# Moving two of sixteen gate blocks from the prompt's part of a decoder layer into the sample's attention

## The chip, the cores and the metric

The kernel runs on one NeuronCore of a Trainium2 chip. The metric is the device time of one execution in microseconds; the kernel before took 1476.8 us (median of three runs, 1475.82 to 1482.26). Engines are called PE (matrix products), DVE (vector), ACT (scalar functions), POOL and SP; in this kernel SP only issues transfers (DMAs), and POOL issues the gathers.

## The reference, cut to what matters

One layer of a decoder is applied to a prompt (256 tokens) and to a sample group (8 sequences of 4 new tokens with 1024 tokens of cache each) with the same weights. The part that matters here:

```
h  = rms_norm(x) * (1 + scale) + shift            # 288 rows of 1024
q, kc, vc, ks, vs, kw, vw, g_nsa, hq, hf, hi, hg, ga, gb = split(h @ w_in)
o_nsa = sparse attention: compressed, selected and window branches, mixed by g_nsa
o_hg  = HGRN2 (4 heads, 128 x 128 state)
m     = sigmoid(ga) * (o_nsa @ w_branch_a) + sigmoid(gb) * (o_hg @ w_branch_b)
out   = m @ w_out
```

After it stand the norm, the residual and a mixture of 32 experts, 4 for each token, whose weights (192 pieces of 2 MB) are all streamed from HBM.

`ga` and `gb` are 1024 columns each. The kernel computes them transposed, in sixteen blocks of 128 columns: block n is `w_in[:, columns of block n]^T @ h^T`, a result of 128 x 288.

## The kernel before, in words

All instructions of each engine are written out in order; engines wait for each other by counting semaphores. What follows is in the order of time.

**Front.** The projection of all columns but `ga` and `gb`, and the compressed keys.

**The sample's attention.** PE transposes cached keys through two banks of PSUM (6 and 7, the "ring", lines 928 to 938) and ACT copies them out. Window scores come first, then selected scores (line 971), which use banks 1 to 4. The selected rows of the cache are gathered by POOL; the last of eight gathers (batch 7, line 2571) waits for `pv_ps` 2, that is, for the window values, because it overwrites a place that the window used. DVE then adds biases and takes maxima, group by group (`softmax`, line 2103; group 0 reads banks 2 and 4 and then raises `s_max` to 4), ACT takes exponentials, DVE divides (`probs` 3), and PE transposes the probabilities (`probs_T`, line 985, five steps) and multiplies them with the cached values (`cached_values`, line 1008) in lines 1104 to 1108. In front of the first of these transposes `probs_T` has `keep_clock`, ten products of the identity with constants whose result nobody reads (line 989).

**The prompt sweep.** A planner in Python (`prompt_steps`, line 165) lays out the steps of the prompt's attention (twelve units), of its HGRN (two tiles of 128 tokens) and of gate blocks into one order, `PROMPT_STEPS`, from assumed durations. Each engine issues its own steps in that order. A gate block is two half blocks of four products each; all go to bank 7. The blocks that the planner finishes before the last other step are `INSIDE` (0 to 9), the rest `LEFT` (10 to 15).

**The tail.** PE runs the blocks in `LEFT` between the steps of the sample's HGRN (lines 1256 to 1286): one block after the inputs, one after the transposes of the keys, one after the heads, one between the two halves of the state updates, and the others after them. Then come two steps of the attention branch (line 1294), the transposes of the HGRN result, and the merge of eight steps (line 1300), after which DVE writes `mT`. SP starts the stream of expert weights when all of `mT` is there (line 704).

**Weights of the gate blocks.** SP loads one piece of 1024 x 128 values (512 KB) for each block, into two places in turn (`load_gate`, line 641); from the third piece on it waits until the block two before has been computed (`gate_ps`). The first twelve are issued in one loop (line 647). Inside it, after the piece of block 5, SP issues a copy of 4064 KB from HBM to HBM, the window state shifted by four tokens (line 650). The remaining pieces are issued between the loads of the branch weights (line 674). SP takes its instructions in order, so a wait there holds all later loads.

Of the kernel before, what the change touches and what calls it, by code (L numbers as in the profile page):

```python
# [20 lines left out]
ACT = mybir.ActivationFunctionType  # L21
# [3 lines left out]
P = 128  # L25
D = 1024
KD = D // P
TP, NB, TS = 256, 8, 4
NS = NB * TS
# [15 lines left out]
ZW = OFF["ga"]  # L45
NZ = -(-ZW // 512)
NGATE = 2 * D // P
# [114 lines left out]
    return sum((i + 1 if branch else 1) for i, branch, _ in UNITS[:u])  # L162


def prompt_steps():


# [24 lines left out]
    for i in range(2):  # L192
# [20 lines left out]
        step("dve", 2.0, "gated", (i,), ("rms", (i,)))  # L213
        step("pe", 1.0, "out", (i,), ("gated", (i,)), ("out_T", (i - 1,)))
        step("act", 0.5, "out_T", (i,), ("out", (i,)))
    for j in range(NGATE):
        for half in range(2):
            step("pe", 2.0, "gates", (j, half), *([("gates", (j, 0))] if half else [("gates_out", (j - 1,))] if j else []))
        step("act", 0.5, "gates_out", (j,), ("gates", (j, 1)))
    emptied = {("out", (i,)): ("out_T", (i,)) for i in range(2)}  # L220
    emptied.update({("gates", (j, 0)): ("gates_out", (j,)) for j in range(NGATE)})
    bank7 = []
    free, done, order = {"pe": 0.0, "act": 0.0, "dve": 0.0}, {}, []
    while todo:
# [14 lines left out]


PROMPT_STEPS = prompt_steps()
_end = max(n for n, s in enumerate(PROMPT_STEPS) if s[0] not in ("gates", "gates_out"))
INSIDE = [j for j in range(NGATE) if PROMPT_STEPS.index(("gates_out", (j,))) < _end]
LEFT = [j for j in range(NGATE) if j not in INSIDE]
PROMPT_STEPS = [s for s in PROMPT_STEPS if s[0] not in ("gates", "gates_out") or s[1][0] in INSIDE]
ORDER = (2, 0, 1)
PIECES = 6 * E
# [2 lines left out]
def build(nc, A, O):  # L250

    with ExitStack() as ctx:
# [207 lines left out]
        osq = ftake(512, HH, DK)  # L460
        sP = [ftake(4 * 256, 4, 256) for _ in range(2)]
        pTp = [ftake(2 * 4 * P, 2, 4, P) for _ in range(2)]
        gate_piece = [ftake(D, KD, P) for _ in range(2)]
        fr["at"] = work0 + 1536 + 512 * 2 + P + 512
        s0 = ftake(NB * HH * DK, NB * HH, DK)
        vm = ftake(NB * DK, NB, DK)
# [102 lines left out]
        def _(sp):  # L569
# [66 lines left out]
            sp.dma_start(lb, A["hg_lb_logits"][0:1].broadcast_to([P, 512])).then_inc(S("ld_hg"), 16)  # L636
            sp.dma_start(oml, A["hg_lb_logits"][1:2].broadcast_to([P, 512])).then_inc(S("ld_hg"), 16)

            sp.wait_ge(S("pv_ps"), 3)
            sp.dma_start(hgn, A["hg_norm"][0:1].broadcast_to([P, P])).then_inc(S("ld_hgn"), 16)  # L640
            def load_gate(j):
                if j >= 2:
                    sp.wait_ge(S("gate_ps"), j - 1)
                sp.dma_start(gate_piece[j % 2], w_in[:, ZW + P * j:ZW + P * j + P].rearrange("(k p) c -> p k c", p=P)
                             ).then_inc(S(f"ld_gp{j % 2}"), 16)

            for j in range(min(NGATE, len(INSIDE) + 2)):
                load_gate(j)
                if j == 5:
                    sp.dma_start(O[7][0, :, 0:WIN - TS].rearrange("b t k g d -> b (t k g d)"),  # L650
                                 A["state_win"][0, :, TS:WIN].rearrange("b t k g d -> b (t k g d)")).then_inc(S("st_out"), 16)
# [1 line left out]
            sp.wait_ge(S("state"), 2)  # L653
            sp.dma_start(s0, A["state_hgrn"][0].rearrange("b h k v -> k (b h) v")).then_inc(S("ld_s0"), 16)
            sp.dma_start(O[8][0, 0].rearrange("h k v -> k h v"), state).then_inc(S("st_state"), 16)
            if len(INSIDE) + 2 < NGATE:
                load_gate(len(INSIDE) + 2)
# [15 lines left out]

            for k in range(8):
                load_branch(k)
                if len(INSIDE) + 3 + k < NGATE:
                    load_gate(len(INSIDE) + 3 + k)
# [68 lines left out]
        def _(pe):  # L746
            mm = nc.tensor.matmul

            def keep_clock(bank, n):

                for _ in range(n):
                    mm(bank[:, 0:256], ident, ctab[:, 0:256], start=True, stop=True)
# [232 lines left out]
            def probs_T(what, n, done):  # L985

                bank = to_ring(what, n)
                if (what, n) == ("sel_p", 0):
                    keep_clock(bank, 10)
                pe.wait_ge(S("probs"), done)  # L990
                src, w, tiles = {"cmp": (sSc, NCMP, 1), "win_p": (sSw, WIN_W, 5), "sel_p": (sSs, SEL_W, 9)}[what]
                for t in range(2 * n, min(2 * n + 2, tiles)):
                    c = min(P, w - P * t)
                    for g in range(G):
                        last = nc.tensor.transpose(bank[0:c, 256 * (t % 2) + P * g:256 * (t % 2) + P * g + P],
                                                   src[:, g, P * t:P * t + c], ident)
                last.then_inc(S("tr_ps"), 1)
# [97 lines left out]
            for i in range(2):  # L1095
                bank = to_ring("pq", 2 * i)
                for r in range(R):
                    last = nc.tensor.transpose(bank[:, P * r:P * r + P], z[:, i, P * r:P * r + P], ident)
                last.then_inc(S("tr_ps"), 1)
                bank = to_ring("pq", 2 * i + 1)  # L1100
                for n, name in enumerate(("ks", "kw")):
                    last = nc.tensor.transpose(bank[:, P * n:P * n + P], zc(i, name, P), ident)
                last.then_inc(S("tr_ps"), 1)
            for t in range(5):
                probs_T("sel_p", t, 3)
                if t:
                    cached_values("sel_p", t - 1)
            cached_values("sel_p", 4)
# [4 lines left out]

            pe.wait_ge(S("tr"), len(RING))
            pe.wait_ge(S("scores_in"), 2)

            def scores(u):
                i, branch, rp = UNITS[u]
# [89 lines left out]
            outs_before = [sum(place_of[("out", (i,))] < place_of[("gates", (j, 0))] for i in range(2)) for j in INSIDE] + [2] * len(LEFT)  # L1208
            gates_before = [sum(place_of[("gates", (j, 0))] < place_of[("out", (i,))] for j in INSIDE) for i in range(2)] + [NGATE]

            def gate_block(j, half):

                if half == 0:
                    pe.wait_ge(S(f"ld_gp{j % 2}"), 16 * (j // 2) + 16)
                    if j:
                        pe.wait_ge(S("gate_out"), j)
                    if outs_before[j]:
                        pe.wait_ge(S("ohT"), outs_before[j])
                for k in range(4 * half, 4 * half + 4):
                    last = mm(banks[7][:, 0:TP + NS], gate_piece[j % 2][:, k], hT[:, k], start=k == 0, stop=k == KD - 1)  # L1220
                if half:
                    last.then_inc(S("gate_ps"), 1)

# [326 lines left out]
        def _(act):  # L1550
# [32 lines left out]
            def exps(src, width, groups, seq):  # L1583
                act.wait_ge(S("s_max"), seq)
                for g in groups:
                    last = fn(src[:, g, 0:width], src[:, g, 0:width], ACT.Exp, bias=sa_max[:, g:g + 1], accum_out=sa_sum[:, g:g + 1])
                last.then_inc(S("s_exp"), 1)
# [92 lines left out]
                nc.scalar.copy(kT[:, :, P * i:P * i + P], bank[:, 0:256].rearrange("p (n t) -> p n t", n=2)).then_inc(S("tr"), 1)  # L1680
            exps(sSs, SEL_W, (0,), 4)
            exps(sSs, SEL_W, (1,), 5)
            for t in range(5):
                probs_out("sel_p", t, 2)
            act.wait_ge(S("pv_ps"), 3)
            nc.scalar.copy(o_ev[:, 0], banks[0][:, 0:P]).then_inc(S("oS"), 1)
            for n in range(2):
                bank = from_ring("out", n)
                for g in range(G):
                    last = fn(onT[DH * g:DH * g + DH, :, 256 + 16 * n:272 + 16 * n].rearrange("p r (b t) -> p r b t", t=TS),  # L1690
                              bank[DH * g:DH * g + DH, 0:P].rearrange("p (b g r t) -> p g r b t", b=4, g=G, r=R)[:, g],
                              ACT.Copy, scale=0.5)
                last.then_inc(S("tr"), 1)
# [64 lines left out]
            def hgrn_result_out(i):  # L1758
# [5 lines left out]
            def gates_out(j):  # L1764
                act.wait_ge(S("gate_ps"), j + 1)
                fn(gates[:, j], banks[7][:, 0:TP + NS], ACT.Tanh, scale=0.5).then_inc(S("gate_out"), 1)
# [844 lines left out]
```

## Time and profile before

| | |
|---|---|
| median of three runs | 1476.8 us |
| profiled execution: its own time | 1477.04 us |
| its span | 1475.2 us |
| PE busy | 1292.9 us |
| DVE / ACT busy | 397.5 / 257.1 us |
| moved by DMA | 503.98 MB |
| mean granted PE clock | 0.954 |

Times in the rows are microseconds from the start of the span. The sample's attention fills roughly 235 to 305, the prompt sweep 305 to 406, the tail 406 to 474, routing and the experts the rest. Where a row names an engine at the end in brackets with an arrow, that is what ended the idle time before the row.

### The profile page before, as it was taken

Reading aid. Unit: us, or ns where it says so; the run is one execution under the profiler, and the core shown is the slowest. Engines: PE = TensorE matmul, PEld = TensorE weight load, DVE = VectorE, ACT = ScalarE, POOL = GpSimd, SP = SyncE. Lnnn points to the kernel's source line nnn. Section 1 sums busy time; section 2 is a strip of 40 time slices with the busy share of each in tenths; the row PEclk is TensorE's granted clock in tenths of the full one; section 3 lists DMA queues with packets and bytes.
Section 4 is the critical chain, followed back from the end, with each engine's and each line's share of the span. In section 5 each row is a group of like instructions: output and inputs, shape, how many; then the busy total and the mean of one; then the engine's idle time right before and its main releaser. Section 6 shows DMA issues by size and latency. Waiting matters only on the chain.

```text
span 1475.2 us, 32485 instructions
## 1 busy us (share of the span) xinstructions
PE 1292.9 (88%) x14329; PEld 639.3 (43%) x14329; DVE 397.5 (27%) x991; ACT 257.1 (17%) x618; POOL 32.1 (2%) x50
## 2 busy tenths in 40 slices
PE   5899998799989978899999679999998669797685
PEld 4554555466767433344444224444443123242232
DVE  5320012458743551112121102121211011121012
ACT  5100005556520310001010001010100000000001
POOL 2000003100000000000000000000000000000000
PEclk9899999999999989899999989999999789899897
DMA  9985764224297999999999999699999999999996
GB/s 283 328 305 200 265 231 168 68 60 156 61 260 254 377 378 424 424 423 426 426 424 422 425 425 425 273 420 414 424 424 425 422 425 425 426 422 424 426 425 252
DMA packets 99043, 503.98 MB, mean 342 GB/s; under 512 B 9473, under 2 KB 38937, under 8 KB 63938
## 3 DMA queue, kind: packets, MB, share of 16 engines
q1 hardware_dynamic: 95234, 483.47, 82.4%
q0 software_dynamic: 3520, 18.90, 3.7%
q8 instruction: 83, 1.36, 0.4%
q10 hardware_dynamic: 192, 0.13, 0.0%
q14 instruction: 14, 0.11, 0.0%
HBM read 496.33 MB, written 10.31 MB: 343 GB/s over the span
## 4 chain that ended last, share of the span: by engine, by line
PE 64%; DMA 26%; DVE 3%; SPq 2%; ACT 2%; issue 1%; POOL 0%; DVEq 0%; ACTq 0%
PE psum L1444 18%; DMA arena<-in_w_up 12%; DMA arena<-in_w_down 11%; PE psum L1463 9%; PE psum L811 4%; PE psum L1220 3%; PE psum L1051 3%; PE psum L1052 3%; PE psum L1477 3%; PE psum L1416 2%; PE psum L1317 2%; PE psum L1430 2%; DMA arena<-in_cache_cmp,arena 2%; SPq L702 2%; PE psum L824 1%
## 5 line engine op out<-in xcount | busy, mean ns | idle before, releaser
L1444 PE MATMUL psum<-arena 128*32 128x512 f32 x3328 | 407.3, 637 | 110.3 <-DMA arena<-in_w_up 95.2
L1444 PEld LDWEIGHTS psum<-arena 128*32 128x32 f32 x3328 | 114.8, 113 | 371.2 <-issue 288.2
L2493 DVE TENSOR_SCALAR arena<-psum 128x256 f32<-128x256 f32 x52 | 22.2, 426 | 678.6 <-PE psum L1430 678.6
L1463 PE MATMUL psum<-arena 128*32 128x256 f32 x3328 | 192.7, 381 | 7.7 <-DMA arena<-in_w_down 7.7
L1463 PEld LDWEIGHTS psum<-arena 128*32 128x32 f32 x3328 | 101.6, 110 | 75.7 <-DMA arena<-in_w_down 12.8
L1880 ACT ACTIVATE arena<-arena 128x256 f32<-128x256 f32 x52 | 21.7, 418 | 572.7 <-DVE arena L2493 572.7
L1220 PE MATMUL psum<-arena 128*128 128x288 f32 x256 | 67.8, 410 | 3.5 <-DMA arena<-in_w_in 2.9
L1477 PE MATMUL psum<-arena 32*128 32x256 f32 x864 | 61.9, 399 | 1.1 <-ACT arena L1889 0.6
L811 PE MATMUL psum<-arena 64*128 64x504 f32 x256 | 56.8, 598 | 1.7 <-DVE arena L1959 1.7
L1430 PE MATMUL psum<-arena 32*32 32x512 f32 x416 | 57.6, 625 | 0.0
L1416 PE MATMUL psum<-arena 128*32 128x256 f32 x832 | 55.9, 386 | 0.0
L1884 ACT COPY arena<-psum 128x256 f32<-128x256 f32 x52 | 19.4, 374 | 203.9 <-PE psum L1463 203.9
L1051 PE MATMUL psum<-arena 128*128 128x512 f32 (+1 forms) x112 | 54.9, 571 | 0.0
L1220 PEld LDWEIGHTS psum<-arena 128*128 128x128 f32 x256 | 46.5, 189 | 18.7 <-DMA arena<-in_w_in 5.2
L1052 PE MATMUL psum<-arena 128*128 128x512 f32 (+1 forms) x112 | 54.1, 564 | 0.0
L1477 PEld LDWEIGHTS psum<-arena 32*128 32x128 f32 x864 | 39.0, 183 | 24.3 <-issue 22.1
L1416 PEld LDWEIGHTS psum<-arena 128*32 128x32 f32 x832 | 21.7, 109 | 52.2 <-issue 43.3
L811 PEld LDWEIGHTS psum<-arena 64*128 64x128 f32 x256 | 25.6, 192 | 30.6 <-issue 30.6
L1484 PE MATMUL psum<-arena 32*32 32x256 f32 x440 | 37.1, 408 | 0.0
L784 PE MATMUL psum<-arena 128*128 128x128 f32 x128 | 21.2, 327 | 16.2 <-DMA arena<-in_cache_cmp,arena 14.9
L1434 PE MATMUL psum<-arena 32*32 32x256 f32 x416 | 34.8, 405 | 0.0
L2065 DVE COPY arena<-psum 128x512 f32<-128x512 f32 (+1 forms) x7 | 4.6, 658 | 109.4 <-PE psum L1057 109.4
(458 smaller groups left out, 1319.5 us busy)
## 6 DMA issues: line engine op xcount, KB each, us to landing
arena<-in_w_up SPq DMA_DIRECT2D x128, 2048.0 KB, 31.7
arena<-in_w_down SPq DMA_DIRECT2D x64, 2048.0 KB, 26.4
arena<-in_w_ada SPq DMA_DIRECT2D x12, 2048.0 KB, 11.3
arena<-in_w_in SPq DMA_DIRECT2D x6, 2048.0 KB, 12.0
arena<-in_w_in SPq DMA_DIRECT2D x16, 512.0 KB, 4.1
arena<-in_state_win SPq DMA_DIRECT2D x4, 1024.0 KB, 11.0
arena<-in_w_out SPq DMA_DIRECT2D x1, 4096.0 KB, 18.1
out<-in_state_win SPq DMA_DIRECT2D x1, 4064.0 KB
```

The costliest lines, as they stand in the source:

```text
L702: sp.dma_start(dst, src).then_inc(S(f"ld_piece{n % R_}"), 16)
L811: last = mm(banks[2 * g + v][:, 0:NB * NCMP], w1[half, s], src, start=s == 0, stop=s == 31)
L1051: mm(b0[:, 0:w], hT[:, k, 0:P], columns(k, 0, w), start=first, stop=final)
L1052: mm(b1[:, 0:w], hT[:, k, P:2 * P], columns(k, 0, w), start=first, stop=final)
L1220: last = mm(banks[7][:, 0:TP + NS], gate_piece[j % 2][:, k], hT[:, k], start=k == 0, stop=k == KD - 1)
L1416: last = mm(banks[1][32 * j:32 * j + SLOT, 256:512], oneslot[:, i], h2r[:, i, 256 * j:256 * j + 256], start=False, stop=i == 1)
L1430: last = mm(banks[0][32 * r:32 * r + SLOT, :], ident[at:at + E, at + e:at + e + 1].broadcast_to([E, SLOT]), bias[at:at + E, :], start=Fals ...
L1434: mm(banks[1][32 * j:32 * j + SLOT, 256:512], oneslot[32 * j:32 * j + NS, 2], h2r[32 * j:32 * j + NS, 2, 0:256], start=True, stop=False)
L1444: last = mm(banks[0][32 * j:32 * j + SLOT].rearrange("p (h c) -> p h c", h=2), xcT[:, q % 2, q // 2], up_cols[n % R_][:, q % 2, j], start= ...
L1463: last = mm(banks[1][32 * j:32 * j + SLOT, 256:512], aT[:, v, 2 * m + h], down_cols[n % R_][:, h, v, j], start=m + v + h == 0, stop=m + v ...
L1477: last = mm(banks[4 + q][:, 256 * i:256 * i + 256], shares[32 * q:32 * q + r, P * i:P * i + P], rows[32 * q:32 * q + r, 0:256], start=star ...
L1484: last = mm(banks[3][at:at + NS, 0:256], shares[32 * q:32 * q + r, TP:TP + NS], rows[32 * q:32 * q + r, 0:256], start=start, stop=stop)
```

## The change

Blocks are renumbered: numbers 0 and 1 are the last two blocks of columns (14 and 15), number j from 2 on is block of columns j - 2. Numbers 0 and 1 (`EARLY = 2`) run in the sample's attention:

- SP loads their pieces into the place of two window batches (`kept`) when `pv_ps` is 2, ahead of the load of `hg_norm`.
- PE drops `keep_clock` there. It computes block 0 in bank 2 before the first transposes of the selected probabilities, and block 1 in bank 4 in four parts, after each of the first four transposing steps. Before a block it waits for its piece and for `s_max` 4.
- ACT applies tanh to block 0 after the last copy of probabilities, and to block 1 after its copy of the first half of the attention's result.
- The planner gets the blocks 2 to 15. It returns the same order as before with each number up by two, so `INSIDE` is 2 to 11 and `LEFT` 12 to 15.
- The loop over pieces starts at `EARLY`; the copy of the window state keeps its condition `j == 5`.

```diff
+EARLY = 2
+def gate_column(j):
+    return (j - EARLY) % NGATE
...
-    for j in range(NGATE):
+    for j in range(EARLY, NGATE):
...
-        gate_piece = [ftake(D, KD, P) for _ in range(2)]
+        gate_piece = [view(kept + D * n, D, KD, P) for n in range(EARLY)] + [ftake(D, KD, P) for _ in range(2)]
+        piece_of = lambda j: gate_piece[j] if j < EARLY else gate_piece[EARLY + j % 2]
...
+            def load_gate(j):
+                if j >= EARLY + 2:
+                    sp.wait_ge(S("gate_ps"), j - 1)
+                c0 = ZW + P * gate_column(j)
+                sp.dma_start(piece_of(j), w_in[:, c0:c0 + P].rearrange("(k p) c -> p k c", p=P)).then_inc(S(f"ld_gp{j % 2}"), 16)
+
+            sp.wait_ge(S("pv_ps"), 2)
+            for j in range(EARLY):
+                load_gate(j)
             sp.wait_ge(S("pv_ps"), 3)
             sp.dma_start(hgn, A["hg_norm"][0:1].broadcast_to([P, P])).then_inc(S("ld_hgn"), 16)
...
-            for j in range(min(NGATE, len(INSIDE) + 2)):
+            for j in range(EARLY, min(NGATE, AHEAD + 2)):
                 load_gate(j)
                 if j == 5:
                     sp.dma_start(O[7][0, :, 0:WIN - TS].rearrange("b t k g d -> b (t k g d)"),
...
-                if (what, n) == ("sel_p", 0):
-                    keep_clock(bank, 10)
...
+            def early_gate(j, ks):
+
+                if ks[0] == 0:
+                    pe.wait_ge(S(f"ld_gp{j % 2}"), 16)
+                    pe.wait_ge(S("s_max"), 4)
+                for k in ks:
+                    last = mm(banks[2 + 2 * j][:, 0:TP + NS], piece_of(j)[:, k], hT[:, k], start=k == 0, stop=k == KD - 1)
+                if ks[-1] == KD - 1:
+                    last.then_inc(S("gate_ps"), 1)
+
+            early_gate(0, range(KD))
             for t in range(5):
                 probs_T("sel_p", t, 3)
+                if t < 4:
+                    early_gate(1, range(2 * t, 2 * t + 2))
                 if t:
                     cached_values("sel_p", t - 1)
...
             pe.wait_ge(S("scores_in"), 2)
+            pe.wait_ge(S("gate_out"), EARLY)
...
             for t in range(5):
                 probs_out("sel_p", t, 2)
+            gates_out(0)
             act.wait_ge(S("pv_ps"), 3)
             nc.scalar.copy(o_ev[:, 0], banks[0][:, 0:P]).then_inc(S("oS"), 1)
+            gates_out(1)
```

## Rows read from the trace of the kernel before

**Rows 1.** The page: busy tenths of the DMA engines, and shares of the chain.
```profile
DMA  9985764224297999999999999699999999999996
PE 64%; DMA 26%; DVE 3%; SPq 2%; ACT 2%; issue 1%; POOL 0%; DVEq 0%; ACTq 0%
```
**Rows 2.** Chain of waits in the sample's attention: start us, us, what.
```profile
278.37 6.07 DMA arena<-in_cache_sel,arena
...
297.33 1.08 PE psum L1015 x32
...
303.59 0.30 DVE arena L2151
```
**Rows 3.** Timeline, same stretch: start us, us, engine line operation, [idle before <-releaser].
```profile
289.86 0.15 DVE L2110 TENSOR_SCALAR arena<-arena 128x1 f32<-128x1 f32 x1
...
290.85 4.58 PE L752 MATMUL psum<-arena 128*128 128x256 f32 x20 [0.47 <-ACT arena L1678]
...
295.92 1.10 PE L995 MATMUL psum<-arena 128*128 128x128 f32 x8 [0.48 <-DVE arena L2117]
...
304.30 0.94 ACT L1690 ACTIVATE arena<-psum 64x64 f32<-64x64 f32 x4 [0.45 <-PE psum L1111]
```
**Rows 4.** Windows: us, busy of PE, PEld, DVE, ACT, POOL, clock, DMA share, GB/s.
```profile
278.40:284.50 6.10, 3.70 (x40) 1.75 (x38) 1.33 (x2) 4.07 (x6) 1.01 (x1) 1.00 0.52 175
304.00:310.50 6.50, 4.97 (x32) 4.04 (x33) 1.72 (x8) 5.47 (x11) 0.00 (x0) 1.00 0.69 171
```
**Rows 5.** The eight gathers of line 2551.
```profile
DMA to landing us min/median/max: 5.9/6.8/10.4
```
**Rows 6.** Chain of waits in the sweep: half blocks of gates (line 1220).
```profile
322.87 2.06 PE psum L1220 x8
...
330.74 2.06 PE psum L1220 x8
...
341.24 2.18 PE psum L1220 x8
...
374.35 1.95 PE psum L1220 x8
```
**Rows 7.** SP's issues; then landings: all pieces (line 644), the one issued at 350.59.
```profile
341.49 0.81 SPq L650 DMA_DIRECT2D out<-in_state_win  x1
350.59 53.67 SPq L644 DMA_DIRECT2D arena<-in_w_in  x6
...
DMA to landing us min/median/max: 3.7/4.1/15.9
...
arena<-in_w_in SPq DMA_DIRECT2D x1, 512.0 KB, 15.9
```
**Rows 8.** Windows, columns as in rows 4: the copy's time, and after it.
```profile
341.50:362.50 21.00, 17.86 (x133) 12.79 (x133) 16.09 (x47) 16.03 (x50) 0.00 (x0) 1.00 0.62 237
362.50:366.60 4.10, 4.10 (x20) 2.40 (x20) 4.03 (x10) 3.03 (x10) 0.00 (x0) 0.59 0.22 64
```
**Rows 9.** Chain of waits in the tail.
```profile
416.09 9.51 DMA arena<-in_w_in
...
429.84 6.29 DMA arena<-in_w_in
436.18 4.16 PE psum L1220 x16
...
445.05 4.13 PE psum L1305 x16
```
**Rows 10.** Timeline: the last state updates on DVE; and the window around them.
```profile
430.90 2.48 DVE L2305 TENSOR_TENSOR arena<-arena,psum 128x512 f32<-128x512 f32 x4 [3.40 <-PE psum L1253]
...
425.00:435.00 10.00, 9.33 (x40) 6.21 (x40) 6.49 (x13) 3.28 (x4) 0.00 (x0) 1.00 0.88 203
```
**Rows 11.** The issue of `w_out` and its landing.
```profile
451.23 4.44 SPq L688 DMA_DIRECT2D arena<-in_w_out  x1
...
arena<-in_w_out SPq DMA_DIRECT2D x1, 4096.0 KB, 18.1
```

More of the change, by code:

```diff
@@ L215, in prompt_steps @@
         step("act", 0.5, "out_T", (i,), ("out", (i,)))
-    for j in range(NGATE):
+    for j in range(EARLY, NGATE):
         for half in range(2):
-            step("pe", 2.0, "gates", (j, half), *([("gates", (j, 0))] if half else [("gates_out", (j - 1,))] if j else []))
+            step("pe", 2.0, "gates", (j, half), *([("gates", (j, 0))] if half else [("gates_out", (j - 1,))] if j > EARLY else []))
         step("act", 0.5, "gates_out", (j,), ("gates", (j, 1)))
     emptied = {("out", (i,)): ("out_T", (i,)) for i in range(2)}
-    emptied.update({("gates", (j, 0)): ("gates_out", (j,)) for j in range(NGATE)})
+    emptied.update({("gates", (j, 0)): ("gates_out", (j,)) for j in range(EARLY, NGATE)})
     bank7 = []
@@ L242 @@
 _end = max(n for n, s in enumerate(PROMPT_STEPS) if s[0] not in ("gates", "gates_out"))
-INSIDE = [j for j in range(NGATE) if PROMPT_STEPS.index(("gates_out", (j,))) < _end]
-LEFT = [j for j in range(NGATE) if j not in INSIDE]
+INSIDE = [j for j in range(EARLY, NGATE) if PROMPT_STEPS.index(("gates_out", (j,))) < _end]
+LEFT = [j for j in range(EARLY, NGATE) if j not in INSIDE]
+AHEAD = EARLY + len(INSIDE)
 PROMPT_STEPS = [s for s in PROMPT_STEPS if s[0] not in ("gates", "gates_out") or s[1][0] in INSIDE]
@@ L637, in _ @@
             sp.dma_start(oml, A["hg_lb_logits"][1:2].broadcast_to([P, 512])).then_inc(S("ld_hg"), 16)
+            def load_gate(j):
[6 more added lines that the diff above has]
+                load_gate(j)
             sp.wait_ge(S("pv_ps"), 3)
             sp.dma_start(hgn, A["hg_norm"][0:1].broadcast_to([P, P])).then_inc(S("ld_hgn"), 16)
[L641 to L645, printed above, removed]
-            for j in range(min(NGATE, len(INSIDE) + 2)):
+            for j in range(EARLY, min(NGATE, AHEAD + 2)):
                 load_gate(j)
@@ L655, in _ @@
             sp.dma_start(O[8][0, 0].rearrange("h k v -> k h v"), state).then_inc(S("st_state"), 16)
-            if len(INSIDE) + 2 < NGATE:
-                load_gate(len(INSIDE) + 2)
+            if AHEAD + 2 < NGATE:
+                load_gate(AHEAD + 2)
             sp.wait_ge(S("p_pv"), len(UNITS))
@@ L675, in _ @@
                 load_branch(k)
-                if len(INSIDE) + 3 + k < NGATE:
-                    load_gate(len(INSIDE) + 3 + k)
+                if AHEAD + 3 + k < NGATE:
+                    load_gate(AHEAD + 3 + k)
             broadcast_rows(gate_rows, 0, "ld_gate")
@@ L1207, in _ @@
             place_of = {s: n for n, s in enumerate(PROMPT_STEPS)}
-            outs_before = [sum(place_of[("out", (i,))] < place_of[("gates", (j, 0))] for i in range(2)) for j in INSIDE] + [2] * len(LEFT)
-            gates_before = [sum(place_of[("gates", (j, 0))] < place_of[("out", (i,))] for j in INSIDE) for i in range(2)] + [NGATE]
+            outs_before = [0] * EARLY + [sum(place_of[("out", (i,))] < place_of[("gates", (j, 0))] for i in range(2)) for j in INSIDE] + [2] * len(LEFT)
+            gates_before = [EARLY + sum(place_of[("gates", (j, 0))] < place_of[("out", (i,))] for j in INSIDE) for i in range(2)] + [NGATE]
             def gate_block(j, half):
@@ L1219, in gate_block @@
                 for k in range(4 * half, 4 * half + 4):
-                    last = mm(banks[7][:, 0:TP + NS], gate_piece[j % 2][:, k], hT[:, k], start=k == 0, stop=k == KD - 1)
+                    last = mm(banks[7][:, 0:TP + NS], piece_of(j)[:, k], hT[:, k], start=k == 0, stop=k == KD - 1)
                 if half:
@@ L1682, in _, with gates_out @@
             exps(sSs, SEL_W, (1,), 5)
+            def gates_out(j):
+                bank = banks[2 + 2 * j] if j < EARLY else banks[7]
+                act.wait_ge(S("gate_ps"), j + 1)
+                fn(gates[:, gate_column(j)], bank[:, 0:TP + NS], ACT.Tanh, scale=0.5).then_inc(S("gate_out"), 1)
             for t in range(5):
                 probs_out("sel_p", t, 2)
+            gates_out(0)
             act.wait_ge(S("pv_ps"), 3)
             nc.scalar.copy(o_ev[:, 0], banks[0][:, 0:P]).then_inc(S("oS"), 1)
+            gates_out(1)
             for n in range(2):
@@ L1762, in hgrn_result_out @@
                 nc.scalar.copy(oh, banks[5][:].rearrange("p (h v) -> p h v", h=HH)).then_inc(S("oh_cp"), 1)
-            def gates_out(j):
-                act.wait_ge(S("gate_ps"), j + 1)
-                fn(gates[:, j], banks[7][:, 0:TP + NS], ACT.Tanh, scale=0.5).then_inc(S("gate_out"), 1)
             steps = {"heads": heads_out, "gates_out": gates_out, "exps": exps_of, "probs_out": probs_T_out, "inputs_out": hgrn_inputs_out, "decays": hgrn_decays,
```

## The prediction

> **What bounds the kernel now.** I read the page first: the DMA line stands at nine tenths or more from the fourteenth slice on, but for one and the last, and the chain that ended last is 64% PE and 26% DMA [rows 1]. So the expert stage, some two thirds of the span, is paced by the stream of expert weights together with PE. The change touches nothing there. That stage starts when the merged rows `mT` are complete (SP waits for them ahead of the first expert piece), its first chunk waits for the routing chain behind them, and later pieces wait for places that PE releases. A shift of `mT` therefore reaches the end one to one. What matters is the stretch before it, which I read in the chain of waits and the timeline.
>
> In the sample's attention the chain runs from the last gather (issued 278.37, landed 6.07 later) over its key transposes to the transposes of the selected probabilities at 295.92, and from 297.33 to 303.59 PE is the chain without a gap [rows 2, 3]. In the prompt sweep PE is again nearly the whole chain, gate half blocks of about 2.0 us among it [rows 6]. Behind the sweep stand six gate blocks beside the sample's HGRN; two of them end a wait for their weights in the chain (416.09 + 9.51 is the transfer of block 13; 429.84 + 6.29 that of block 15, which starts at 436.18), and then come the branch products and, at 445.05, the merge [rows 9].
>
> **Part 1: keep-clock out, block 0 in: 0.** Before, 20 matmuls that nobody reads ran from 290.85 for 4.58 us, ending 0.48 before the probabilities were there at 295.92 [rows 3]. Block 0 has 16 instructions, 2 x 1.95 to 2 x 2.06 = 3.9 to 4.1 us [rows 6]. It waits for its piece (early, below) and for the first selected maximum, written at 289.86 + 0.15 [rows 3]; behind that wait on PE stand only the transposes that wait for 295.92 anyway. It ends by about 295.0. Were that cover gone, it would cost its 4 us.
>
> **Part 2: block 1 among the selected products: +3.9.** It is issued in four parts of four instructions between transposes and products. The only gap there is 297.33 - (295.92 + 1.10) = 0.31 us [rows 3]; after it PE is the chain [rows 2]. So 16 instructions cost 3.9 to 4.1, and four changes between shapes add at most 0.1 each (2.06 against 1.95 in the sweep), less 0.3: 3.6 to 4.2, I take 3.9. On ACT, tanh of block 0 falls before the last product is done, and tanh of block 1 goes into the 0.45 us in which ACT waited for the last transposes [rows 3]; a copy of a like width on ACT takes about as long: 0, at most 0.4. The new wait for two `gate_out` ahead of the prompt's scores is met by then: 0.
>
> **Part 3: two pieces beside the last gather: +1.2.** SP now issues two pieces of 512 KB when `pv_ps` reaches 2, the semaphore on which POOL issues the gather; both go out near 278.3. The gather kept the DMA engines busy for 0.52 x 6.1 = 3.2 us; two pieces and the small norm load took 0.69 x 6.5 = 4.5 us [rows 4]. PE waited for that gather, so a delay is paid in full. Below: 0 (it cannot land earlier for this). Above: the pieces' 4.5 us go first as a whole; they start some 1.4 earlier (0.3 in the issue, and 1.0 that POOL takes to write the gather's descriptors [rows 4]), so the gather is pushed by 3.1. The other gathers ran beside weight slabs and landed in a median of 6.8 against 6.07, +0.7 [rows 2, 5]. I take 1.2, near that row, since a piece has 1024 small packets. The rest of SP's queue at that point (norm load, piece 2) waits for `pv_ps` 3 as before.
>
> The Trainium skill (DMA: Bandwidth & Descriptors, "Queues, rings and completion order") says that each DMA engine takes turns between the rings of SP and POOL, packet by packet. By it the gather would get about half of each engine while both run, and the sum would be nearer to +3 here than to 0; no row of this trace shows the two together with pieces this small.
>
> **Part 4: the copy of the window state moves forward: +9.1 and +2.0.** This is the step that I think decides. The sweep's order is the same, with each block's number up by two: ten blocks inside, so they and the prompt's steps cost the same. But in SP's loop the 4064 KB copy from HBM to HBM is still issued after `load_gate(5)`. Before, that was the sixth block of the sweep and went out at 341.49; now block 5 is the fourth of the sweep. Its load waits for `gate_ps` 4, of which two are the early blocks, so it goes out when the sweep's second block is done, 322.87 + 2.06 = 324.9, and the copy at 325.3, 16.2 us earlier [rows 6, 7]. Times here and below are on the axis of before; all shift by parts 2 and 3.
>
> What the copy does to a piece behind it can be read: the piece issued at 350.59 took 15.9 us, until 366.5, where the others have a median of 4.1. In the copy's time the engines are busy at a share of only 0.62 over 21 us, and the piece still landed 4 us after the copy's end [rows 7, 8]. Before, this cost nothing, because that block starts at 374.35 [rows 6]. The landing is 25.0 us after the copy's issue. Now the piece behind the copy is that of the sweep's fifth block: issued when its third is done (330.74 + 2.06 = 332.8), landing at 325.3 + 25.0 = 350.3. PE comes to that block at 341.24 [rows 6]: a wait of 9.1 us. Behind it on PE stand the values and scores of all later prompt units and the HGRN products; DVE and ACT wait for those, and what they hold (one exponential, one set of factors) is under 2 us of work that was already beside PE. So 7 to 10 of it come through. I take 9.1. The next piece lands soon behind it and is needed only a block later.
>
> After such a wait PE's clock is down: from 362.5 on, after a stretch in which PE had been busy for 17.9 of 21 us with its idle time at the end, the granted clock was 0.59 over 4.1 us [rows 8]. That is 1.2 GHz in place of 2.4 GHz for some 3.4 us, which loses 1.7 where PE is the chain; after a longer pause I allow 0 to 3.4 (missed, or twice as long) and take 2.0.
>
> The row leaves two readings: the piece is held in order behind the copy, or it merely shares. The Trainium skill (DMA: Bandwidth & Descriptors, "Queues, rings and completion order" and "Why a DMA increments its semaphore by 16 and not by 1") says that on each engine the descriptors of one queue are taken in order, and that a copy with eight outer rows uses eight engines. By it the eight halves of the piece stay behind the copy and my 9.1 stands; by plain sharing there would be no wait and a sum of -1.4. The 15.9 us agree with the rule.
>
> **Part 5: two blocks less behind the sweep: -6.5.** Four blocks remain, with the same places between the HGRN steps, and the fourth's piece (416.09 + 9.51) is issued as before. The last two go, with their waits (436.18 is the start of the last); their tanh too, and no table load with them. Late next are the state updates: DVE's last ends at 430.90 + 2.48 = 433.38, and the branch products wait for it [rows 10]. They began when 436.18 + 4.16 = 440.3 was done [rows 9]: at most 6.9 gained, less 0.1 for the wake-up. The branch weights are late after that. SP issues them without waits for gate blocks, and engines at a share of 0.88 [rows 10] lose two pieces, 4.5 us of work [rows 4]: if DMA alone were the limit, 4.5 would be the gain. I take 6.5, near the first, because 0.88 leaves idle time to be filled too. `w_out` takes 18.1 from 451.23, until 469.3 [rows 11]; it is needed after the merge, 445.05 + 4.13 and six steps of 3.9 = 472.6 [rows 9]. It must come 3 us sooner too; its issue hangs on the sample state's store, which goes out 2 us earlier (at 433.4) behind two pieces less. I take no wait there.
>
> **Sum.** 0 + 3.9 + 1.2 + 9.1 + 2.0 - 6.5 = +9.7 us on the profiled execution's 1477.04 (span 1475.2 and 1.8 around it), which lies 0.2 above the median 1476.8: 1486.7.
>
> **Rivals.** A, not slower: the piece passes beside the copy on engines that it leaves free (share 0.62), and PE does not wait at 341.24. Then 3.9 + 1.2 - 6.5 = -1.4: 1475.6. It decides as soon as the piece lands within 8.4 us of its issue. Against it: 15.9. Chance 0.14.
> B: the wait is there, but the sweep takes part of it back, since PE is idle for 21.0 - 17.9 = 3.1 us later in it [rows 8] where ACT and DVE are late, and the clock stays high: 3.9 + 1.2 + (9.1 - 3.1) - 6.5 = +4.6, 1481.6. Against it: those idle times hang on work that PE must first release. Chance 0.14.
> C: the engines are the limit twice, the gather 3.1 late and the tail giving 4.5: 3.9 + 3.1 + 11.1 - 4.5 = +13.6, 1490.6. Chance 0.10.
> The forecast: 0.62.
>
> About 0.5%, 7.4 us, can be told from no change. The forecast's own range is 1482 to 1490; with B, most of C and part of A it is 1477 to 1491. Slower by over 0.5% (above 1484.2): nine tenths of the forecast, C and a tenth of B, 0.67. Faster by over 0.5%: 0.02. Within: 0.31.
>
> **What would show it.** Right: a wait of PE for `in_w_in` of 7 to 10 us at the fifth gate block of the sweep, its piece landing over 15 us after issue; a low granted clock after it; branch products about 7 us sooner after the fourth remaining block; about 4 us more between the selected transposes and the last selected product. Wrong: no such wait (A); a gather landing 9 us after issue, or a wait for branch weights (C). A run at 1476 would say that part 4 is wrong, whatever else holds.

## The result, and the profile after

The kernel before took 1476.45 us in the median of 4 runs (1475.82 to 1482.26), the changed one 1493.38 us in the median of 4 (1492.92 to 1495.83). The ratio is 1.0122, with a 95% interval of 1.0092 to 1.0152: the change costs 1.2%. The forecast was 1486.7 us within 1477 to 1491. The sign and the step that decides are as forecast; the size is 6.7 us too small, and the time lies outside the range.

The profiled execution of the changed kernel has a span of 1491.1 us, 15.9 above the one before. The sections below follow these 15.9 us along the chain of waits. First the sample's attention; columns are start us, us, what:

```profile
276.99 9.14 DMA arena<-in_cache_sel,arena
288.82 3.62 PE psum L993 x8
...
300.48 0.63 PE psum L1005 x4
301.11 0.97 PE psum L1120 x4
...
311.62 0.30 DVE arena L2178
...
314.33 5.42 PE psum L764 x12
...
322.37 2.14 PE psum L1244 x8
```

Against [rows 2] the gather takes 9.14 in place of 6.07 us. The key products behind it (L993, eight instructions) take 3.62 us; in the kernel before, eight of the same kind took 1.92 us from 286.31. The selected transposes (L1005) now have block 1 (L1120) between them, and from their start to the output copies of the sample's heads pass 311.62 - 300.48 = 11.14 us, against 303.59 - 295.92 = 7.67 [rows 2, 3]. Then the keep-clock products ahead of the prompt (L764, twelve instructions) take 5.42 us. In the timeline of the kernel before, the same products are the second of these rows; the first is what followed the gather's landing there:

```profile
284.49 1.09 PE L968 MATMUL psum<-arena 128*128 128x128 f32 x8 [1.33 <-DMA arena<-in_cache_sel,arena]
...
305.85 2.86 PE L752 MATMUL psum<-arena 128*128 128x256 f32 x12
```

The timeline of PE after shows block 0 (16 instructions of L1120 from 294.69) ending in the idle time ahead of the probabilities, and both waits for transfers; in brackets is the idle time ahead of a row and what ended it:

```profile
286.18 1.97 PE L980 MATMUL psum<-arena 128*128 128x128 f32 x8 [4.40 <-DMA arena<-in_cache_sel,arena]
...
294.69 4.06 PE L1120 MATMUL psum<-arena 128*128 128x288 f32 x16
300.48 0.63 PE L1005 MATMUL psum<-arena 128*128 128x128 f32 x4 [1.73 <-DVE arena L2144]
...
361.26 3.85 PE L1244 MATMUL psum<-arena 128*128 128x288 f32 x8 [9.71 <-DMA arena<-in_w_in]
```

The windows (columns as in [rows 4]) give the granted clock that belongs to the long rows:

```profile
286.00:292.00 6.00, 5.14 (x16) 2.11 (x16) 0.00 (x0) 1.18 (x2) 0.00 (x0) 0.51 0.00 0
314.00:318.00 4.00, 4.00 (x13) 3.25 (x13) 1.66 (x8) 3.44 (x4) 0.00 (x0) 0.50 0.95 256
...
361.30:365.30 4.00, 4.00 (x10) 2.68 (x12) 0.00 (x0) 0.00 (x0) 0.00 (x0) 0.59 0.05 14
```

Half of full speed is 1.2 GHz in place of 2.4: it stands behind the gather's wait, ahead of the prompt, and behind the sweep's wait.

The sweep, as SP's issues (timeline) and then as the chain:

```profile
336.22 0.81 SPq L662 DMA_DIRECT2D out<-in_state_win  x1
343.28 10.68 SPq L652 DMA_DIRECT2D arena<-in_w_in  x2
```
```profile
343.28 17.94 DMA arena<-in_w_in
...
361.26 3.85 PE psum L1244 x8
```

The piece behind the copy lands at 343.28 + 17.94 = 361.22, 25.0 us after the copy's issue, which is what [rows 7] gave for before (25.3 in before_copy_early and 24.7 in gather_first, below). PE waits 9.71 us for it. In the tail (chain) the fourth block is followed by what was forecast as late next, the state updates of DVE and then the branch products:

```profile
434.99 6.96 DMA arena<-in_w_in
...
442.00 4.16 PE psum L1244 x16
...
447.23 4.09 PE psum L1244 x16
...
452.43 2.47 DVE arena L2332 x4
...
455.04 4.13 PE psum L1314 x16
...
460.00 2.18 PE psum L1329 x8
```

The sum along the chain, in us. "Sample state's load" is SP's issue at the sweep's end (406.36 before, 428.07 after); the merge is L1305 before and L1329 after; the first expert products start at 538.67 and 552.58.

| stretch | before | after | difference | forecast |
|---|---|---|---|---|
| start to the gather's issue | 278.37 | 276.99 | -1.4 | 0 |
| the gather's transfer | 6.07 | 9.14 | +3.1 | +1.2 |
| its landing to the first selected transpose | 11.48 | 14.35 | +2.9 | 0 |
| selected transposes and products | 7.67 | 11.14 | +3.5 | +3.9 |
| from there to the first gate block of the sweep | 8.31 | 10.75 | +2.4 | 0 |
| sweep, the wait and the block behind it taken out | 92.28 | 92.14 | -0.1 | 0 |
| the wait, and the half block behind it | 2.18 | 13.56 | +11.4 | +11.1 |
| sample state's load to the merge | 38.69 | 31.93 | -6.8 | -6.5 |
| merge to the first expert products | 93.62 | 92.58 | -1.0 | 0 |
| experts to the end | 936.5 | 938.5 | +2.0 | 0 |

The sum of the unrounded rows is +15.9. Three rows that the forecast had at 0 or too low carry the miss: the gather's transfer (1.9 more than forecast) and the two stretches behind it (+5.3); the other rows together take 1.0 of it back. The first and the last rows, where the programs do the same, show how far two executions differ anyway.

The gather's +3.1 has two parts. These are the landing of the gather in the kernel before, in the changed kernel and in keep_gather (below, where the two pieces go out beside it as well), each row (of the views of DMA issues) with its microseconds at the end; then, for the changed kernel, what each DMA queue moved from 283.9 to 284.0 and from 284.2 to 286.2 (queue: packets, MB, share of the engines):

```profile
arena<-in_cache_sel,arena POOLq DMA_INDIRECT x1, 6.1
...
arena<-in_cache_sel,arena POOLq DMA_INDIRECT x1, 9.1
...
arena<-in_cache_sel,arena POOLq DMA_INDIRECT x1, 7.6
```
```profile
q8 instruction: 1, 0.02, 67.9%
...
q0 software_dynamic: 1, 0.00, 0.1%
```

In the trace of the changed kernel fifteen of the gather's sixteen completion signals arrive within 7.7 us of its issue. The sixteenth, the one packet of queue 0 in the second row, goes out only at 8.1, as a load of 16 KB of instructions (queue 8) ends that had begun at 7.0, and it arrives at 9.14. In copy_later and copy16 the same stands at the same times. In keep_gather and keep_later2 that load begins when the gather's packets are done, and the gather lands at 7.62 and 7.66. So the two pieces by themselves cost the gather about 1.6 us, and a last signal that comes late another 1.5. That this signal stood on the same DMA engine as the instruction load is inferred from the times; the rows do not name the engine.

### The profile page after: what moved, and what is told of

The parts are those of the page before. It is cut to its first block, busy times and chain, and to the rows that moved or that the text cites. A ratio compares the mean times of both kernels' runs of the same rounds, so it can differ in the third digit from the quotient of the medians.

```text
span 1491.1 us, 32445 instructions
## 1 busy us (share of the span) xinstructions
PE 1290.1 (87%) x14309; PEld 638.0 (43%) x14309; DVE 397.8 (27%) x991; ACT 254.8 (17%) x616; POOL 32.1 (2%) x50
## 4 chain that ended last, share of the span: by engine, by line
PE 64%; DMA 27%; DVE 3%; SPq 2%; ACT 2%; issue 1%; POOL 0%; DVEq 0%; ACTq 0%
PE psum L1468 18%; DMA arena<-in_w_down 14%; DMA arena<-in_w_up 9%; PE psum L1487 9%; PE psum L823 4%; PE psum L1061 3%; PE psum L1062 3%; PE psum L1244 3%; PE psum L1501 3%; PE psum L1440 2%; PE psum L1341 2%; DMA arena<-in_cache_cmp,arena 2%; PE psum L1454 2%; DMA arena<-in_w_in 2%; SPq L714 2%
## 5 line engine op out<-in xcount | busy, mean ns | idle before, releaser
L1244 PE MATMUL psum<-arena 128*128 128x288 f32 x224 | 61.2, 419 | 11.1 <-DMA arena<-in_w_in 10.7
L1244 PEld LDWEIGHTS psum<-arena 128*128 128x128 f32 x224 | 41.8, 195 | 24.4 <-DMA arena<-in_w_in 12.0
L823 PEld LDWEIGHTS psum<-arena 64*128 64x128 f32 x256 | 25.3, 186 | 29.3 <-issue 29.3
## 6 DMA issues: line engine op xcount, KB each, us to landing
arena<-in_w_out SPq DMA_DIRECT2D x1, 4096.0 KB, 17.9
```

The costliest lines, as they stand in the source:

```text
L823: last = mm(banks[2 * g + v][:, 0:NB * NCMP], w1[half, s], src, start=s == 0, stop=s == 31)
L1244: last = mm(banks[7][:, 0:TP + NS], piece_of(j)[:, k], hT[:, k], start=k == 0, stop=k == KD - 1)
```

## The experiments

The runs came in three sets, each with runs of the kernel before on its own chip: a median of 1477.89 us (23 runs) for copy_later, before_copy_early, gather_first and both, 1477.74 us (30) for keep_gather, copy16, early_one and both_fill, and 1475.79 us (17) for keep_later2. Ratios are to these. They differ by up to 2.1 us, so across sets the distance to the kernel before is the fairer comparison; the changed kernel's is +16.9 us.

**copy_later** takes the sweep's wait out: the copy goes out after the same block of the sweep as before the change.

```
-                if j == 5:
+                if j == 5 + EARLY:
```

> The changed kernel, with the copy of the window state issued after piece 7 (the sixth of the sweep, as before) instead of piece 5. Theory (the piece behind the copy is held for 25.0 us after the copy's issue): PE's wait of 9.7 us at the sweep's fifth block and the half-rate block after it (+1.7) are gone, 1493.4 - 11.4 = 1482.0. Rival (the copy only moves DMA work about, and another late piece takes its place): 1488 or more.

Measured: 1480.41 us (10 runs), ratio 1.0018 [1.0002, 1.0034]. The copy went out at 350.96, and PE waited for no piece in the sweep. The gather took 9.15 us as in the changed kernel. Between the medians, 13.0 of the 16.9 us go with this one line. The profiled execution, the slowest of the ten, shows less: the sample state's load comes 428.07 - 419.31 = 8.8 us earlier, of 11.4 that the wait and the half block behind it had cost. Its sweep takes 97.6 us against 94.5 before, with windows at a clock of 0.86, 0.83 and 0.83 (350 to 360, 370 to 380, 400 to 410).

**before_copy_early** does that one thing to the kernel before: no early block, only the copy two issues earlier.

```
-                if j == 5:
+                if j == 3:
```

> The kernel before, with nothing changed but that the copy of the window state is issued after piece 3 instead of piece 5, the place in the sweep that the change gives it. Theory: PE waits about 9.1 us at the sweep's fifth block for a piece that lands 25.0 us after the copy's issue, and its clock costs 1.7: 1476.5 + 10.8 = 1487.3. Rival (the wait in the changed kernel comes of the renumbered pieces or the early blocks): no change, 1476.5.

Measured: 1488.88 us (4 runs), ratio 1.0078 [1.0055, 1.0101], 11.0 us above before. Its chain and its windows:

```profile
330.09 17.84 DMA arena<-in_w_in
347.97 4.21 PE psum L1220 x8
```
```profile
344.00:352.00 8.00, 4.03 (x8) 2.53 (x8) 0.00 (x0) 0.00 (x0) 0.00 (x0) 0.50 0.23 66
```

PE waited 9.6 us, and the half block behind ran at half clock, 4.21 in place of 2.18 us: 9.6 + 2.0 = 11.6. The wait needs nothing of the change but the copy's place, and the median agrees with the price of 9.1 + 2.0. In the profiled execution the sweep is 109.7 - 94.5 = 15.2 us longer: some 3.6 us more went in it behind that half block, where the windows at 350 to 360, 370 to 380 and 400 to 410 have a clock of 0.67, 0.83 and 0.83.

**gather_first** keeps the changed kernel, but SP issues the two early pieces only when the last gather has landed.

```
             sp.wait_ge(S("pv_ps"), 2)
+            sp.wait_ge(S(landed[7]), 32)
             for j in range(EARLY):
```

> The changed kernel, with SP issuing the two early pieces only when the last gather has landed; the copy still early. Theory (the pieces delay the gather by 3.1, and the longer idle time lowers PE's clock right after it, +2.8, and again ahead of the prompt's HGRN, +2.4): the gather is back at about 6.1 us and all 8.3 go, 1485.1. Rival (the clock is low for another reason, such as the keep-clock products that are gone): only 3.1 go, 1490.3. Rival 2 (the pieces now come too late for block 0): a new wait of PE for a piece near 290.

Measured: 1488.63 us (4 runs), ratio 1.0073 [1.0049, 1.0098], 4.8 us below the changed kernel's median (6.2 by the distance to before) and between the two expectations. Its chain:

```profile
275.96 6.04 DMA arena<-in_cache_sel,arena
```

The gather is back at 6.04 us, and from its issue to the first selected transpose pass 293.57 - 275.96 = 17.6 us (before 17.55, changed 23.49). The granted clock is 1.00 from 282 to 306 and then 0.66 for 4 us ahead of the prompt (the twelve keep-clock products take 4.47 us). PE waited for neither of the two pieces: they are in time although they start 6 us later. The sweep's wait is there as before, 9.0 us. The first gate block of the sweep comes 7.5 us sooner after the gather's issue than in the changed kernel; 0.8, 1.0 and 1.5 us of it are given back in the sweep, in the tail and behind the first expert products.

**both** has the two edits together.

> Both edits. Theory: what is left of the change is +3.5 in the selected loop and -6.8 in the tail, 1476.5 - 3.3 = 1473.2. Rival (clock low anyway): 1478.4.

Measured: 1473.08 us (12 runs), ratio 0.9975 [0.9959, 0.9991], where 1473.2 was expected. That is 15.6 us below gather_first and 7.3 below copy_later. In its chain the gather takes 5.80 us, the first selected transpose comes 17.4 us after its issue, and the windows at 286 to 292 and 304 to 310 have the clock at 1.00:

```profile
276.31 5.80 DMA arena<-in_cache_sel,arena
...
293.68 0.63 PE psum L1006 x4
```
```profile
286.00:292.00 6.00, 5.49 (x28) 4.04 (x27) 3.87 (x13) 4.96 (x8) 0.00 (x0) 1.00 0.21 50
304.00:310.00 6.00, 4.60 (x46) 3.30 (x38) 0.82 (x2) 4.95 (x10) 0.00 (x0) 1.00 0.55 142
```

With both costs gone the idea of the change wins a quarter of a per cent. The terms for it were +3.9 in the attention and -6.5 in the tail; the profiled execution has +3.5 and -6.1, and a sweep 1.6 us longer than before (96.07 against 94.46).

**keep_gather** is to part the clock from the transfer: the changed kernel, with matmuls that nobody reads on PE while it waits for the gather. The pieces still go out beside it. The transfer did not stay the same, though: it took 7.62 us, as said above.

```
             def selected_keys(b):
+                if b == 7:
+                    keep_clock(to_ring("sel", 14), 9)
                 pe.wait_ge(S(landed[b]), 32)
```

> The changed kernel, with nine keep-clock products (nobody reads them) ahead of the wait for the last gather, some 4 us of work in an idle time of 4.3; the loads, the gather and the copy as in the change. Theory (the idle time lowers the clock): the key transposes and selected products after the gather run at full rate, 2.8 less, 1490.6, and 1488.2 if the low stretch near 314 goes with it. Rival (the delay is all in the transfers): no change, 1493.4.

Measured: 1493.38 us (5 runs, 1484.89 to 1499.79), ratio 1.0101 [1.0069, 1.0134]. A row of the timeline, the chain and windows:

```profile
285.55 1.04 PE L982 MATMUL psum<-arena 128*128 128x128 f32 x8
```
```profile
287.31 1.91 PE psum L995 x8
...
297.02 0.63 PE psum L1007 x4
```
```profile
286.00:292.00 6.00, 4.80 (x30) 2.68 (x29) 2.62 (x8) 2.73 (x6) 0.00 (x0) 1.00 0.00 0
314.00:318.00 4.00, 4.00 (x31) 3.48 (x32) 1.85 (x14) 3.29 (x13) 0.00 (x0) 1.00 0.11 26
356.00:366.00 10.00, 9.87 (x57) 6.45 (x56) 3.03 (x17) 2.41 (x11) 0.00 (x0) 0.67 0.01 3
378.00:384.00 6.00, 3.89 (x20) 2.50 (x22) 5.90 (x11) 5.15 (x15) 0.00 (x0) 0.78 0.01 3
404.00:412.00 8.00, 8.00 (x55) 5.73 (x55) 3.36 (x8) 2.12 (x4) 0.00 (x0) 0.79 0.25 68
```

Locally it does what it should: the key products take 1.91 in place of 3.62 us, and the first gate block starts 316.40 - 276.84 = 39.56 us after the gather's issue in place of 45.31, 5.75 less. The last gather's transposes start 0.5 us sooner after its issue (285.55 - 276.84 = 8.71 in place of 9.19); from their start to the first selected transpose pass 297.02 - 285.55 = 11.47 us, against 14.30 in the changed kernel and 11.43 before. So 2.8 us of the first stretch behind the gather were the clock's. The other 2.4 us ahead of the prompt are gone too, where the clock stood at 1.00 as well. But the sweep took 426.32 - 316.40 = 109.9 us in place of 105.8: its wait is still 9.6, and more of it ran at a low clock. The total shows no gain that could be told from the spread of these five runs; the expected one was missed.

**keep_later2** tests that reading: the same fill, and the copy in its later place, so that the sweep has no wait.

> The changed kernel with two edits at once: the copy of the window state goes out after the same block of the sweep as before the change (as in copy_later, which gave 1480.4), and nine matmul pairs that nobody reads run ahead of the wait for the last gather (as in keep_gather), so that PE is not idle there. The gather is still beside the two early pieces. If the low granted clock behind the gather's wait is what cost +5.2 us between the gather's landing and the first gate block of the sweep, and if keep_gather's local gain of 5.75 us vanished in the low clock behind the sweep's wait, then without that wait it must reach the end: 1480.4 - 5.75 = 1474.7 us, and the gather's transfer still 9.1 us. Rival: what is won ahead of the prompt is given back in the sweep whatever the wait there, as a low stretch at another place: 1480.4, with a row of windows at a granted clock near 0.5 to 0.6 between 330 and 420.

Measured: 1477.62 us (12 runs), ratio 1.0008 [0.9991, 1.0025], between the two expectations: 2.8 below copy_later's median, but only 0.7 by the distance to before (+1.8 against +2.5), and the intervals overlap. The gather took 7.66 us and not the 9.1 expected. In the profiled executions, 1480.0 in span against 1484.4, the first gate block came 5.0 us earlier than in copy_later (316.69 against 321.69), the sample state's load 3.4 earlier (415.90 against 419.31). So locally the gain is there and part of it is given back in the sweep, where three windows are low; that any of it reaches the total is not shown:

```profile
350.00:360.00 10.00, 10.00 (x68) 7.00 (x67) 7.05 (x26) 6.40 (x24) 0.00 (x0) 0.83 0.54 218
...
390.00:400.00 10.00, 10.00 (x67) 7.26 (x64) 5.28 (x10) 3.57 (x7) 0.00 (x0) 0.82 0.20 54
400.00:410.00 10.00, 9.62 (x47) 7.17 (x45) 3.55 (x6) 3.00 (x6) 0.00 (x0) 0.84 0.20 52
```

**copy16** asks whether the piece is held by the copy's own length on half of the engines. The changed kernel, with the copy as 16 rows of 31 tokens and a rest of 12 tokens.

```
-  sp.dma_start(O[7][0, :, 0:WIN - TS]..., A["state_win"][0, :, TS:WIN]...)
+  sp.dma_start(O[7][0, :, 0:496].rearrange("b (c t) k g d -> c b (t k g d)", c=16),
+               A["state_win"][0, :, TS:TS + 496].rearrange(..., c=16)).then_inc(S("st_out"), 16)
+  sp.dma_start(O[7][0, :, 496:WIN - TS]..., A["state_win"][0, :, TS + 496:WIN]...)...
```

> The changed kernel, with the copy in the same early place, but cut into 16 rows of 31 tokens for each sequence and a small rest, so that its slowest dimension is 16 and not 8. Theory (the copy goes through eight engines and holds what is queued behind it there): with 16 engines it takes half as long, the piece behind it lands some 15 us after the copy's issue and not 25, PE does not wait for it at the sweep's fifth block, 1493.4 - 11.4 = 1482.0. Rival (the copy is bound by HBM, whatever the engines): 1493.

Measured: 1489.14 us (10 runs, 1478.87 to 1491.00; the profiled one is the slowest), ratio 1.0064 [1.0045, 1.0083]. The timeline of SP, the chain and the windows:

```profile
337.40 0.68 SPq L662 DMA_DIRECT2D out<-in_state_win  x1
338.13 0.73 SPq L664 DMA_DIRECT2D out<-in_state_win  x1
```
```profile
344.47 10.28 DMA arena<-in_w_in
...
354.79 3.55 PE psum L1246 x8
```
```profile
338.00:344.00 6.00, 6.00 (x43) 4.45 (x42) 5.83 (x17) 2.43 (x9) 0.00 (x0) 1.00 1.07 375
...
354.80:358.00 3.20, 3.20 (x8) 2.04 (x8) 1.04 (x3) 0.11 (x2) 0.00 (x0) 0.61 0.32 92
358.00:368.00 10.00, 10.00 (x65) 6.96 (x66) 5.68 (x25) 5.14 (x22) 0.00 (x0) 0.78 0.01 2
```

The engines are now at a share of about 1 during the copy (0.62 in [rows 8]); the piece lands at 354.75, 17.35 us after the copy's issue in place of 25.0, and PE waits 2.0 us in place of 9.7. The wait is thus set by how long the copy occupies the engines that the piece needs. The Trainium skill (DMA: Bandwidth & Descriptors, "Why a DMA increments its semaphore by 16 and not by 1") says that the outermost dimension decides how many engines share a transfer; by that rule sixteen rows use sixteen engines where eight use eight, and the two shares agree. The time was expected at 1482.0 and came out 7 higher (6 by the distance to before): of the 7.7 us less of waiting only 105.8 - (426.25 - 323.48) = 3.0 came through the sweep. A wait of 2.0 us was still followed by a low clock, 3.2 x 0.39 + 10 x 0.22 = 3.4 us of it in the last two rows.

**early_one** starts from both, moves one block only (block 0), and leaves none among the selected products. `EARLY = 1`, and without these lines:

```
-                if t < 4:
-                    early_gate(1, range(2 * t, 2 * t + 2))
...
-            gates_out(1)
```

> Both corrections (gather first, copy later), and only block 0 early: no block among the selected products, five blocks behind the sweep. Theory: the front costs nothing (-3.5 against both corrections alone), the tail loses one block and the wait for the last piece, 5.2 of the 6.8: 1476.5 - 5.2 = 1471.3, and 1.9 under two early blocks. Rival (the tail's limit is the transfers, so that one block less gives half of it): 1473.

Measured: 1472.48 us (12 runs), ratio 0.9962 [0.9945, 0.9979], the lowest ratio of all kernels here, though its interval overlaps that of both, and between the two expectations. From the first selected transpose to the output copies pass 9.2 us, 1.95 less than in both but not the 3.5 that block 1 had cost, and a window there is low (8 x 0.21 = 1.7). And in the tail another wait is next, that for the branch weights:

```profile
294.00:302.00 8.00, 7.13 (x114) 5.39 (x114) 0.40 (x1) 2.57 (x8) 0.00 (x0) 0.79 0.01 2
```
```profile
420.00 4.18 PE psum L1243 x16
...
429.07 11.98 DMA arena<-in_w_branch_b
```

**both_fill** starts from both and puts more of block 1 into the idle time of PE ahead of the probabilities.

```
             early_gate(0, range(KD))
+            early_gate(1, range(3))
...
-                    early_gate(1, range(2 * t, 2 * t + 2))
+                    early_gate(1, (range(3, 5), range(5, 6), range(6, 7), range(7, 8))[t])
```

> Both corrections and two early blocks, with the first three of block 1's eight products moved ahead of the selected transposes, where PE is idle for 1.7 us, the others 2, 1, 1, 1 after the transposing steps. Theory: of the 3.5 us in the selected loop 1.5 go, 1471.6. Rival (bank 4 is not free in time, or the first transposes are held): 1473 or more.

Measured: 1474.89 us (12 runs), ratio 0.9974 [0.9958, 0.9991]. The stretch fell from 11.14 to 303.91 - 294.23 = 9.68 us, but the windows 306 to 310 and 420 to 424 stand at 0.57 and 0.68, where both had 1.00 in the first. Nothing of the 1.5 us can be seen in the time, which is in the rival's range.

## Why the prediction was right, and where it failed

**Part 1, block 0 under the idle time: right.** It ran from 294.69 to 298.75, and PE was idle for 1.73 us behind it. It costs nothing.

**Part 2, +3.9: right.** +3.5 in the trace. That early_one won back only 1.95 of it locally fits the low window there.

**Part 3, +1.2: the step that failed**, in its size and in what it left out. It set PE's wait for the gather at the delay of the transfer alone, +1.2; the runs showed +3.1 for the transfer and +5.3 in the two stretches behind it, of which 2.8 are shown to be a low clock that the longer wait brought.

The transfer first. The bounds were 0 and 3.1, and the trace has +3.07. The upper bound let the pieces' engine time go ahead of the gather as a whole, and that is not what happened: from 280.9 to 284.1 both queues moved data, the gather's at a share of 82.4% and the pieces' at 21.0%, and in keep_gather and keep_later2 the gather came only 1.6 us late beside the same pieces. The rest is the late last signal, which neither bound was made of. So 1.2 was near what the pieces cost by themselves, the rival C had the right number for the transfer by luck, and gather_first shows that without the pieces both parts are gone: 6.04 us. The Trainium skill (DMA: Bandwidth & Descriptors, "Queues, rings and completion order") has the engines take turns between SP's and POOL's rings; the trace agrees in that both moved data at once, but the sum nearer to +3 than to 0 that the prediction worked out by it came about only with the late signal.

**What no part had: the clock behind the gather.** The prediction priced the low clock only behind the sweep's wait, and behind the gather's at nothing, without a reason. The same thing happened there: PE's idle time ahead of the gather's landing grew to 4.40 us, from 1.33 before (where eight transposes at 284.49 ended it), and the clock fell to half for 286 to 292; later it was at half for 314 to 318, with no idle time of more than 0.92 us in the 10 us ahead. Together +5.3 us, more than the transfer itself. For the first stretch keep_gather shows the cause: with PE filled the clock stays at 1.00, and from the start of the last gather's transposes on 2.8 us come back. Why the second one fell is not shown: with PE filled at the gather it stayed at 1.00 in keep_gather, and in gather_first, where no wait of PE there is longer than 1.7 us, it fell to 0.66 all the same.

**Part 4, +9.1 and +2.0: right.** The piece at the fifth block of the sweep, landing 17.9 us after issue and 25.0 after the copy; 9.71 us of waiting and 3.85 - 2.18 = 1.67 us of clock; then no more of it in the sweep (62.96 against 62.93 us for the rest). Rivals A and B fall: the piece did not pass, and in the changed kernel nothing was absorbed. before_copy_early has the same price alone by its median, copy_later has the time without it.

**Part 5, -6.5: right.** -6.76, and DVE's state updates are late next, as named. The sweep's wait did not decide that: in both and copy_later, which have none, DVE's updates are late next as well, and the stretch is 6.1 and 5.2 us shorter than before. The branch weights were late only in early_one.

**The sum.** Forecast 0 + 3.9 + 1.2 + 9.1 + 2.0 - 6.5 = 9.7. With the two terms as measured, 3.1 for the gather and 5.3 for the clock: 3.5 + 3.1 + 5.3 + 9.7 + 1.7 - 6.8 = 16.5, against 15.9 by the profiled executions and 16.9 by the medians. The range ended at +14 because its upper case allowed the gather's worst but no clock behind it.

## What to carry to other kernels

Count a block's number in every loop that hangs on it: the early blocks were cheap, and the line `if j == 5` that nobody touched cost 11 us, since a long copy in one queue moved ahead of pieces that PE needs. Where a wait of the engine that makes the path grows, price the clock behind it each time, not only at the largest wait; here the wait grew by 3.1 us and 2.8 more went to the clock right behind it. And do not start a prefetch in the same moment as the transfer for which the path is waiting: held back until the gather's landing it was in time, and both corrections together turned a ratio of 1.0122 into 0.9975.

## What the runs showed of the hardware

Windows of 4 to 10 us with a low granted clock turned up in every trace looked at closely, and not only behind long idle times: at 314 to 318 in the changed kernel (0.50), at 306 to 310 in gather_first (0.66), both_fill and early_one (0.57 in both), at 350 to 360 and 390 to 410 in keep_later2 (0.82 to 0.84, as much as half of full speed for a third of the 10 us). Each costs some 1.5 to 3 us (5.42 - 2.86 = 2.6 for the keep-clock products of the changed kernel, 10 x 0.17 = 1.7 for one of the long ones), about what these edits were to win, and they stand elsewhere in each kernel. They are what the traces offer for why 5.75 us won ahead of the prompt (keep_gather) and 5.0 (keep_later2) cannot be seen in the medians. What decides where they fall stays open.

An indirect gather of 6.07 us beside two loads with small packets took 9.14, 9.17 and 9.15 us in three kernels, 7.62 and 7.66 in two, and 5.80 to 6.14 in six where these came later or not at all. The steps are as steady as the times: in the three, one of its sixteen completion signals left only when a 16 KB load of instructions of 1.1 us was over, and the whole DMA counted as landed by it. PE waited those 1.5 us with all but that signal there. Why the load met the gather in three kernels and missed it in two is not shown; it began 7.0 us after the gather's issue in the three and 7.2 to 7.3 after it in the two.
